# A convolution by Fourier transform: one load requested earlier, and three groups of results stored straight into the next stage's buffer

## The reference

```
z = short_conv(u @ w_in + b_in, conv_w, conv_b)
x0, x1, v = jnp.split(z, 3, axis=-1)
s = v * x1
g = hyena_filter(...)                                  # (2L, D), normalised
y = irfft(rfft(s, n=2L) * rfft(g, n=2L), n=2L)[:, :L]
y = (y + s * skip) * x0
return y @ w_out + b_out
```

## Time and profile before

| | |
|---|---|
| three runs, median (lowest to highest) | 2584.03 us (2579.1 to 2587.91) |
| profiled execution: its span | 2581.9 us |
| profiled execution: its own time | not given apart from the span |
| VectorE, ScalarE, GpSimd, share of the span busy | 44%, 25%, 27% |
| chain that ended last, by line | L1182 70%, L522 5%, no other line over 2% |
| DMA over the span | 84 GB/s mean |

### The profile page before, as it was taken

The page is one execution under the profiler, slowest core; times in us unless marked ns, Lnnn a source line. Parts: engine busy times, 40 slices in busy tenths (PEclk is TensorE's granted clock), DMA queues, the critical chain, the costliest instruction groups (busy, mean ns, idle before and its releaser), DMA issues.

```text
span 2581.9 us, 29118 instructions
## 1 busy us (share of the span) xinstructions
PE 2456.0 (95%) x11358; PEld 1971.7 (76%) x11358; DVE 1132.0 (44%) x1181; ACT 642.4 (25%) x776; POOL 702.7 (27%) x394
## 2 busy tenths in 40 slices
PE   7998789979999999999999799999999999999996
PEld 5884466647888888888888598989898787778885
DVE  6646453335347314641336772626262223430533
ACT  4114523334120000000112363636363101111001
POOL 2331023321333333333334211212121232323331
PEclk9999999999999999999999899999999999999998
DMA  4111253483123112211211031111112421112231
GB/s 146 49 47 60 113 190 139 156 240 124 41 97 116 48 48 99 96 65 49 65 49 58 33 114 38 59 38 59 38 59 73 171 84 60 57 49 65 89 118 70
DMA packets 69967, 217.59 MB, mean 84 GB/s; under 512 B 6662, under 2 KB 16584, under 8 KB 69642
## 3 DMA queue, kind: packets, MB, share of 16 engines
q1 hardware_dynamic: 57002, 178.88, 21.2%
q10 hardware_dynamic: 12896, 37.75, 3.9%
HBM read 171.52 MB, written 45.09 MB: 84 GB/s over the span
## 4 chain that ended last, share of the span: by engine, by line
PE 90%; DVE 5%; ACT 2%; issue 2%; DMA 1%; ACTq 0%; SPq 0%; DVEq 0%
PE ps L1182 70%; PE ps L522 5%; PE ps L1332 2%; DVE T L1861 2%; PE ps L1394 1%; PE ps L1451 1%; PE ps L1373 1%; PE ps L1252 1%; PE ps L569 1%; PE ps L1262 1%; PE ps L589 1%; PE ps L551 1%; PE ps L590 1%; PE ps L588 1%; PE ps L1339 1%
## 5 line engine op out<-in xcount | busy, mean ns | idle before, releaser
L1182 PE MATMUL ps<-H,whi 128*128 128x512 f32 x4000 | 1084.1, 393 | 19.6 <-DVE H L1928 11.5
L1182 PEld LDWEIGHTS ps<-H,whi 128*128 128x128 f32 x4000 | 751.5, 189 | 189.9 <-issue 22.3
L1136 POOL CAST whi<-wraw 128x1024 fp32r<-128x1024 f32 x190 | 201.5, 1060 | 1753.1 <-PE ps L1182 883.7
L1182 PE MATMUL ps<-H,wlo 128*128 128x512 f32 x2000 | 618.0, 390 | 0.0
L1138 POOL TENSOR_TENSOR wlo<-wraw,whi 128x1024 fp32r<-128x1024 f32 x194 | 489.5, 2523 | 58.4 <-ACT whi L656 43.1
L1182 PEld LDWEIGHTS ps<-H,wlo 128*128 128x128 f32 x2000 | 377.0, 189 | 79.2
L1182 PE MATMUL ps<-A,whi 128*128 128x512 f32 x1472 | 396.4, 391 | 5.1 <-DVE A L2236 4.9
L1182 PEld LDWEIGHTS ps<-A,whi 128*128 128x128 f32 x1472 | 277.6, 189 | 63.8 <-issue 5.3
L1182 PE MATMUL ps<-A,wlo 128*128 128x512 f32 x736 | 227.5, 390 | 0.0
L1182 PEld LDWEIGHTS ps<-A,wlo 128*128 128x128 f32 x736 | 138.8, 189 | 29.0
L2120 DVE TENSOR_TENSOR T<-ps,T 128x1024 f32<-128x1024 f32 x22 | 26.9, 1224 | 155.8 <-PE ps L1182 155.8
(11 more groups left out here) (339 smaller groups left out, 2515.3 us busy)
## 6 DMA issues: line engine op xcount, KB each, us to landing
wraw<-in_panels SPq DMA_DIRECT2D x181, 512.0 KB, 3.5
mw<-in_modp SPq DMA_DIRECT2D x24, 512.0 KB, 3.5
g<-gsp SPq DMA_DIRECT2D x16, 512.0 KB, 2.6
wraw<-g SPq DMA_DIRECT2D x16, 512.0 KB, 5.7
bs<-s SPq DMA_DIRECT2D x16, 512.0 KB, 4.7
y<-yi ACTq DMA_DIRECT2D x32, 256.0 KB, 4.8
kf<-in_kfft SPq DMA_DIRECT2D x16, 320.0 KB, 3.3
X<-in_xT SPq DMA_DIRECT2D x4, 1024.0 KB, 10.5
```

What stands on the lines that cost most here:

```text
L1136: nc.gpsimd.tensor_copy(whi[:, s, :, :], wraw[:, s, :, :]).then_inc(hi_made, 1)
L1182: last = mm(p[:, c * step:(c + 1) * step], w[:, ws, k, :], operand(act, a, k, c * step, step), start=(q == 0 and w is whi and a == 0), sto ...
```

## The change

The last three groups (13 to 15) are stored by ACT straight into `YB`, and SP reads back groups 8 to 12 in one part. PE waits for those last stores itself, for halves 29 to 31. Apart from that, the request for the second group's filter rows moves from behind `signal_in(1)` to the signal stage, ahead of the stores of sets 14 and 15.

```diff
-BACK = (8, 12, 16)
+BACK = (8, 13)
@@ SP, after the store of set 13
                     for g in range(2):
                         matrices(g)
+                    filter_rows(1)
             for m in range(N2 - 4, N2):
                 sp.wait_ge(*sa_out(m))
@@ SP, first three groups
                 signal_in(g)
                 matrices(g + 2)
                 if g:
-                    filter_rows(g)
+                    if g > 1:
+                        filter_rows(g)
@@ SP, after the last group's loads
-            for part in (1, 2):
-                y_stored(BACK[part])
-                for k in range(4):
-                    y_back(part, k)
+            y_stored(BACK[1])
+            for k in range(4):
+                y_back(1, k)
@@ PE, inverse stage, first job of a column block
-                        pe.wait_ge(x_in[k], 64)
+                        pe.wait_ge(x_in[k], 16 * (1 + len(BACK)))
+                        if k == 0:
+                            for n in range(2 * GROUPS - 3, 2 * GROUPS):
+                                pe.wait_ge(y1_out[n % 3], y1_stored(n))
@@ ACT, store of half n
-                act.dma_start(y1.rearrange("p n t -> (p n) t")[g * P:(g + 1) * P, 512 * c:512 * c + 512], yi[n % 3][:, :]
-                              ).then_inc(y1_out[n % 3], 16)
+                if g < BACK[-1]:
+                    act.dma_start(y1.rearrange("p n t -> (p n) t")[g * P:(g + 1) * P, 512 * c:512 * c + 512], yi[n % 3][:, :]
+                                  ).then_inc(y1_out[n % 3], 16)
+                else:
+                    act.dma_start(YB[8 * g:8 * g + 8, :, 512 * c:512 * c + 512], yi[n % 3][:, :]
+                                  ).then_inc(y1_out[n % 3], 16)
```

## The result

The changed kernel takes 2588.78 us (median of 15 runs) against 2584.38 us (15 runs): ratio 1.0019, 95% interval 1.0011 to 1.0027. The medians lie 4.4 us apart, the ratio says 4.9; it is slower, inside the 0.3% that the prediction called no change, but not on the side of its -2.0. The profiled execution has a span of 2589.4 us, 7.5 more than before; it ran in 2591.22 us.

The account below looks back on a forecast made before the run. TensorE is busy 95% of the span, so only its pauses at two places could change the time. -8.7 us at the first and +6.7 at the second gave -2.0, from 2584.0 to 2582.0 us, range 2567 to 2597.

Parts of the forecast that it names:

- A: Start of the spectrum stage: requesting the second group's filter rows earlier removes PE's 7.54 us pause; 8.7 us saved.
- The signal rows' request: Start of the spectrum stage: SP's request moves from 370.54 to about 372.2, 1.7 us; rows 0.4 us late at most.
- the weight panel: Start of the spectrum stage, half 3: the panel is late next, split until 385.0, and PE waits 0.7 us for it.
- let the gain come through whole: Later groups of the spectrum stage: they keep the 8.7 us, since the remaining waits are tied to events moving together.
- B: End of the spectrum stage: direct stores into YB replace the last reading back; PE starts the inverse 6.7 us later.
- B's price of one store: End of the spectrum stage: a 256 KB store into 8 partitions takes 5.0 us, plus about 2.1 us of latency.
- B's sharing: End of the spectrum stage: four stores queue from 563.1, mostly overlapped with the reading back, which adds 1.8 us.
- The reading of the earlier trace that spoke against blocking: End of the spectrum stage: stores of halves 28 to 30 ran beside part 1's loads, hardly cutting their 208 GB/s.
- The rival nearest in mechanism: End of the spectrum stage: crowded stores block other traffic, times add; inverse starts 18.1 us late, total 2593.4 us; chance 0.20.
- The forecast's own sign at B: Ahead of the inverse: PE's wait is ended by a direct store, 15 us after the last copy of yi.
- Rival 1: Stores at the spectrum stage's end aren't held up at their destination: PE starts 4.9 us sooner, 2570 us; chance 0.30.
- The slow clock: Start of the inverse: the clock at 0.50 from 578 to 583 stays, for the pause before it stays.

Follow-up runs that it names:

- the three-load rounds: Kernel of DMAs alone: three loads issued by SyncE, without or with one 256 KB store; loads to partitions 64 to 103: 17.9 us alone, 20.3 with store.

## Why the prediction was wrong, point by point

**A** was right in mechanism and nearly in size: -8.7 forecast, -9.6 and -7.5 measured alone. Within it, two terms were too small. The signal rows' request slid by 2.9 us like for like (374.37 against 370.54, less the 0.9) and not 1.7: SP's own request for the first filter rows took 1.89 us to issue, and the store of set 15 landed after 8.97 us. So PE did wait, 1.7 us. What came last next was the weight panel, as said, at 387.20 where 385.1 + 0.9 = 386.0 was forecast. The text also let the gain come through whole; the traces of the early request alone show 8.2 and 8.5 us at the last result and 6.1 and 6.9 at the inverse, for the last store lands later behind the same loads.

**B's price of one store** was right: 5.0 us forecast at the upper bound; 4.4 us measured at 59 GB/s, with 2.2 of latency where 2.1 was taken.

**B's sharing** is the step that failed. The text said that the stores of halves 28 to 31 start fresh at 563.1, "mostly overlapped", and added 1.8 us for the read back: 23.9 us from half 28's issue to the last landing. The changed kernel has 29.6, and B cost +11.6 us where +6.7 was forecast. The trace with the read back put behind the stores splits the difference. There it is 23.7 and not 22.1, for the two stores of group 13 were still in the queue behind part 0, and half 28 landed 11.0 us after issue instead of 7.1; later stores, 4.2 us apart where 5.0 was taken, gave some of that back. The read back beside the stores cost 5.9 us instead of 1.8. Its loads were mis-sized too: 3.1 us each at 208 GB/s, but a load into 40 partitions takes 5.2 (7.3 less the latency; the three-load rounds say (17.9 - 7.3) / 2 = 5.3), against 2.5 for 32.

The reading of the earlier trace rows that spoke against blocking was wrong. The stores of halves 28 to 30 were issued from 563.05 on, beside the loads of part 1, but the queues show that they didn't run beside them. In the kernel before, from 562 to 569, then from 569 to 575:

```profile
q1 hardware_dynamic: 1447, 1.44, 110.1%
...
q10 hardware_dynamic: 575, 1.05, 49.7%
q1 hardware_dynamic: 473, 0.46, 29.4%
```

Up to 569 ScalarE's queue (q10) moved nothing. The loads weren't cut because the stores waited for them. After that, stores to DRAM were done in a few us (1.05 MB in 6), so the waiting cost little; four stores into 8 neighbours take 17.6 us of moving at 4.4 each.

**The rival nearest in mechanism** is the second one: the times add, and copies of `yi` wait for stores. Its price, 18.1 us late at the inverse, was too high: it added six whole stores to the loads one behind the other. Like for like the inverse starts 4.1 us later than before where A alone brought it 6.1 and 6.9 earlier, so B made it 10 to 11 late, which is nearer to the forecast's 6.7 than to the rival's price. PE's wait of 20.4 us also lies between the two, under the 25 that the rival asked for. The forecast's own sign at B, a start 15 us after the last copy of `yi`, came true (15.6 after 569.7); that doesn't bear it out, since the last copy itself was late by its wait of 6.2 us for a store. Rival 1 is out (6.6 us a store alone).

**The slow clock.** I let it stay as it was. The inverse's first 48 products took 1.4 us more (13.52 against 12.15). The length of the pause alone doesn't settle that: with one group direct PE waited 15.6 us and they took 12.15 again, with the early request alone 10.3 us and 13.04. Why is open.

The sum with measured terms: -7.5 to -9.6 for A, +11.6 for B, +2.0 to +4.1 us, against +4.9 by the ratio of the whole. All are ratios, each uncertain by 2 to 4 us.

## What to carry to other kernels

Before a buffer in memory is cut out and results go straight to their place, ask how many partitions, and which, one store reaches: 8 neighbours took 256 KB at 59 GB/s, and that time came on top of the transfers around it, also of those to other partitions. So look at the stores already queued and at those that share the queues, and add before you overlap. Whether transfers that seem to run side by side do so, the packets of each queue tell. Where the arrangement of a buffer is free (here a constant's row order), try the rows of one transfer four partitions apart; sixteen apart was slower again. A pause that one early request removes is worth looking for first: it gave 0.3 to 0.4% for one moved line.

## What the runs showed of the hardware that I had not expected

- A store into 8 neighbouring partitions adds its time to DMAs on another issuer's queue to other partitions: 9.8 us became 14.3 beside loads into partitions 0 to 63. It waited behind them, and held up their last 41 packets of 1584.
- Stores issued behind loads may move nothing until the loads are nearly through, though they are on another issuer's queue: none from 562 to 569 in the kernel before.
- A load into 40 partitions takes nearly twice the time of one into 32: three of them 17.9 against 9.8 us, for a quarter more bytes.
- 8 partitions sixteen apart (4.8 us) are slower than 8 four apart (4.0) and faster than neighbours (6.6). The Trainium skill, "SBUF — State Buffer", section "Door 1: The DMA port swizzle", gives four ports, eight and two for these three; the order agrees, the times not in proportion.
